# Two layers of a hybrid backbone step on one core: convolution taps dealt anew, pooled sums scaled by ScalarE, row tiles turned through two pairs of PSUM banks

## The reference

```python
h = _rms(x, norm1_g) * (1.0 + sc1) + sh1          # modulation from w_mod
u = h @ w_in                                      # 1024 -> 2048
qa, ka, va, pool_in, glu_in, qd, kd, vd = split(u)
# B: for windows w = 2, 4, 8, 16 on 64 channels each
mean = (cs[:, hi + 1] - cs[:, lo]) / (hi - lo + 1)
o_b = concat((mean - pool_in) @ pool_w) * pool_scale
# C: 31 taps along the tokens, per channel
g = a * sigmoid(gate)
y = conv(g, conv_dw_w, width=31) + conv_dw_b
o_c = silu(layer_norm(y)) @ conv_pw
x = x + g1 * (concat(o_a, o_b, o_c, o_d) @ w_out)  # o_a, o_d: attention
```

## Time and profile before

| | |
|---|---|
| median of 3 runs | 2039.86 us |
| lowest and highest | 2038.81 and 2039.9 us |
| the profiled execution | 2038.71 us |
| its span | 2036.9 us |
| mean granted TensorE clock | 0.935 |
| busy: PE, PEld, DVE, ACT, POOL | 85%, 67%, 29%, 25%, 14% |
| moved | 533.77 MB, 262 GB/s in the mean |

### The profile page before, as it was taken

The page is one execution under the profiler, slowest core; times in us unless marked ns, Lnnn a source line. Parts: engine busy times, 40 slices in busy tenths (PEclk is TensorE's granted clock), DMA queues, the critical chain, the costliest instruction groups (busy, mean ns, idle before and its releaser), DMA issues.

```text
span 2036.9 us, 65158 instructions
## 1 busy us (share of the span) xinstructions
PE 1726.2 (85%) x29816; PEld 1373.7 (67%) x29816; DVE 582.2 (29%) x971; ACT 518.6 (25%) x1286; POOL 289.2 (14%) x292
## 2 busy tenths in 40 slices
PE   4999889984999888888769968999379998989894
PEld 2555466453999888888735535655279998888884
DVE  2168466242111101011123774742501110101011
ACT  2122366111221212121221315641122121212212
POOL 1166200000000000000011680000000000000001
PEclk7999889986999999999979978999589999999997
DMA  9220911247999999999950228012369999999996
GB/s 391 105 83 0 364 59 43 83 171 256 376 388 392 395 389 400 389 400 390 400 200 1 83 92 329 2 63 93 117 243 381 395 393 388 400 388 399 388 396 257
DMA packets 136647, 533.77 MB, mean 262 GB/s; under 512 B 5888, under 2 KB 6976, under 8 KB 136320
## 3 DMA queue, kind: packets, MB, share of 16 engines
q1 hardware_dynamic: 121616, 482.53, 60.3%
q0 software_dynamic: 6336, 21.63, 4.5%
q10 hardware_dynamic: 8624, 28.61, 3.8%
HBM read 508.33 MB, written 24.41 MB: 262 GB/s over the span
## 4 chain that ended last, share of the span: by engine, by line
PE 44%; DMA 32%; SPq 9%; DVE 7%; issue 4%; ACT 2%; POOL 2%; ACTq 0%; POOLq 0%; DVEq 0%; PEldq 0%; PEld 0%
DMA ring<-in_exp_w_down 16%; PE PS L752 13%; SPq L345 9%; PE PS L672 7%; DMA ring<-in_exp_w_up 5%; PE PS L506 4%; DMA x_rows<-arena 4%; DMA arena<-xn_rows,arena 4%; DMA ring<-in_w_mod 3%; PE PS L565 3%; PE PS L582 2%; PE PS L477 2%; PE PS L478 2%; DVE arena L1201 1%; PE PS L411 1%
## 5 line engine op out<-in xcount | busy, mean ns | idle before, releaser
L752 PE MATMUL PS<-arena,ring 128*64 128x80 f32 x24576 | 898.2, 233 | 97.4 <-DMA ring<-in_exp_w_up 41.6
L752 PEld LDWEIGHTS PS<-arena,ring 128*64 128x64 f32 x24576 | 876.7, 137 | 121.3 <-DMA ring<-in_exp_w_up 48.4
L1039 ACT ACTIVATE arena<-PS,modB,modA 128x64 f32<-128x64 f32 (+1 forms) x544 | 153.5, 421 | 405.6 <-PE PS L738 405.6
L1560 POOL DMA_INDIRECT x_rows<-arena x32 | 45.7, 1429 | 756.6 <-DVE arena L1410 756.6
L672 PE MATMUL PS<-ring,H 128*128 128x512 f32 x320 | 139.2, 593 | 0.0
L1397 DVE TENSOR_TENSOR arena<-arena,PS 128x320 f32<-128x320 f32 x64 | 31.4, 490 | 326.1 <-PE PS L752 326.1
L672 PEld LDWEIGHTS PS<-ring,H 128*128 128x128 f32 x320 | 60.0, 190 | 71.9 <-issue 71.7
L506 PE MATMUL PS<-H,ring 128*128 128x512 f32 x192 | 104.6, 628 | 3.4 <-ACT H L826 3.4
L1051 ACT ACTIVATE arena<-PS 128x320 f32<-128x320 f32 x32 | 14.0, 438 | 346.0 <-PE PS L752 346.0
L1201 DVE SCALAR_TENSOR_TENSOR arena<-arena,par 128x655 f32<-128x655 f32 x72 | 99.0, 1375 | 2.2
L1268 DVE TENSOR_REDUCE stat<-PS 128x2 f32<-128x1280 f32 (+1 forms) x54 | 75.5, 1400 | 62.0 <-PE PS L552 53.5
(11 more groups left out here) (191 smaller groups left out, 1733.9 us busy)
## 6 DMA issues: line engine op xcount, KB each, us to landing
ring<-in_exp_w_down SPq DMA_DIRECT2D x64, 2048.0 KB, 26.5
ring<-in_exp_w_gate SPq DMA_DIRECT2D x64, 2048.0 KB, 24.6
ring<-in_exp_w_up SPq DMA_DIRECT2D x64, 2048.0 KB, 25.0
ring<-in_w_mod SPq DMA_DIRECT2D x24, 2048.0 KB, 18.3
ring<-in_w_in SPq DMA_DIRECT2D x8, 2048.0 KB, 27.6
ring<-in_w_out SPq DMA_DIRECT2D x4, 2048.0 KB, 22.6
arena<-x_rows ACTq DMA_DIRECT2D x15, 512.0 KB, 6.7
x_rows<-arena ACTq DMA_DIRECT2D x10, 512.0 KB, 2.6
```

Source lines behind the costliest of these rows:

```text
L752: last = mm(PS[r0:r0 + HD, b0 + j // 4, (j % 4) * CAP:(j % 4 + 1) * CAP], halves[:, s, k * 512 + (j % 4) * P + r0:k * 512 + (j % 4) * P + ...
L1039: last = do(xeT[:, jj, c0:c1], PS[:, 6 + part, j * CAP + c0:j * CAP + c1], ACT.Identity, bias=modB[:, 1, v, jj:jj + 1], scale=modA[:, 1, v ...
```

## The change

Four things. The taps (c) and products (k) are dealt anew in TAKE_ORDER; their number stays 38 and 24. In layer 1 the first pooling moves behind the root of tile 4. The scaling of the pooled sums goes from GpSimd to ScalarE, which waits for the sums (pool_sums) and answers (pool_scaled). Row tiles 1 and 3 of layer 0 and tile 1 of layer 1 are turned into banks 5 and 6, and a tile waits only for the last use of its own pair.

```diff
+        pool_sums, pool_scaled = sem("pool_sums"), sem("pool_scaled")
...
-                uses = [0]
+                uses, last_use = [0], {0: 0, 5: 0}
...
                     uses[0] += 1
+                    last_use[0] = uses[0]
...
                     pe.wait_ge(n_xn, NT * l + t + 1)
-                    banks01(l)
+                    if last_use[XBANK[l][t]]:
+                        pe.wait_ge(b0_evac, 10 * l + last_use[XBANK[l][t]])
+                        pe.wait_ge(b1_evac, 10 * l + last_use[XBANK[l][t]])
+                    uses[0] += 1
+                    last_use[XBANK[l][t]] = uses[0]
                     for j in range(KD):
-                        last = tr(PS[:, j // 4, (j % 4) * P:(j % 4 + 1) * P], xt[t][:, j * P:(j + 1) * P],
+                        last = tr(PS[:, XBANK[l][t] + j // 4, (j % 4) * P:(j % 4 + 1) * P], xt[t][:, j * P:(j + 1) * P],
...
+                def scale_pool(i):
+                    act.wait_ge(pool_sums, 2 * l + i + 1)
+                    for rows, src in ((slice(0, HD), wa), (slice(HD, P), wb)):
+                        last = do(poolD3[rows, i, :], src[rows, PAD:PAD + OUTW], ACT.Copy, scale=invw[rows, i:i + 1])
+                    last.then_inc(pool_scaled, 1)
...
+                    elif kind == "p" and n == 0:
+                        scale_pool(0)
...
+                scale_pool(1)
                 take_mod(l, 3, mix_rows[1], 0)
...
-                    for rows, src in ((slice(0, HD), wa), (half, wb)):
-                        last = G.tensor_scalar(poolD3[rows, i, :], src[rows, PAD:PAD + OUTW], invw[rows, i:i + 1],
-                                               None, ALU.mult)
-                    link(last)
+                    pool.sem_inc(pool_sums, 1)
+                    reach(pool_scaled, 2 * l + i + 1)
...
-               ("p", 0), ("f", 2), ("f", 3), ("c", 5), ("f", 4), ("f", 5), ("m", 2), ("k", 6), ("c", 8), ("j", 0),
-               ("k", 5), ("c", 6), ("q", 0), ("j", 1), ("k", 5), ("c", 6), ("q", 1), ("j", 2), ("k", 5), ("c", 6),
-               ("q", 2), ("j", 3), ("k", 3), ("c", 6), ("q", 3), ("j", 4), ("c", 1), ("f", 1), ("p", 1), ("q", 4)),
+               ("p", 0), ("f", 2), ("f", 3), ("c", 7), ("f", 4), ("f", 5), ("m", 2), ("k", 6), ("c", 11), ("j", 0),
+               ("k", 5), ("c", 5), ("q", 0), ("j", 1), ("k", 5), ("c", 5), ("q", 1), ("j", 2), ("k", 5), ("c", 5),
+               ("q", 2), ("j", 3), ("k", 3), ("c", 5), ("q", 3), ("j", 4), ("f", 1), ("p", 1), ("q", 4)),
...
-               ("z", 0), ("j", 1), ("f", 2), ("f", 3), ("c", 2), ("q", 1), ("c", 6), ("f", 4), ("f", 5), ("m", 2),
-               ("k", 7), ("c", 9), ("j", 2), ("k", 9), ("c", 8), ("f", 0), ("q", 2), ("j", 3), ("k", 8), ("c", 6),
-               ("q", 3), ("p", 0), ("j", 4), ("c", 4), ("f", 1), ("p", 1), ("c", 3), ("q", 4)))
+               ("z", 0), ("j", 1), ("f", 2), ("f", 3), ("c", 2), ("q", 1), ("c", 11), ("f", 4), ("f", 5), ("m", 2),
+               ("k", 9), ("c", 13), ("j", 2), ("k", 9), ("c", 7), ("f", 0), ("q", 2), ("j", 3), ("k", 6), ("c", 5),
+               ("q", 3), ("j", 4), ("p", 0), ("f", 1), ("p", 1), ("q", 4)))
...
+XBANK = ((0, 5, 0, 5, 0), (0, 5, 0, 0, 0))
```

More of the change, by code:

```diff
@@ L825, in step_x @@
                     for j in range(4):
-                        last = do(H[:, j, t * P:(t + 1) * P], PS[:, 0, j * P:(j + 1) * P], ACT.Identity,
+                        last = do(H[:, j, t * P:(t + 1) * P], PS[:, XBANK[l][t], j * P:(j + 1) * P], ACT.Identity,
                                   bias=modB[:, 0, v, j:j + 1], scale=modA[:, 0, v, j:j + 1])
@@ L1134, in step_x @@
                     for j in range(4):
-                        last = V.tensor_scalar(H[:, 4 + j, t * P:(t + 1) * P], PS[:, 1, j * P:(j + 1) * P],
+                        last = V.tensor_scalar(H[:, 4 + j, t * P:(t + 1) * P], PS[:, XBANK[l][t] + 1, j * P:(j + 1) * P],
                                                modA[:, 0, v, 4 + j:5 + j], modB[:, 0, v, 4 + j:5 + j],
```

## The result

The changed kernel took 2012.26 us in the median of four runs (2006.2 to 2018.0), the kernel before 2039.34 beside it: a ratio of 0.9873, 95% interval 0.986 to 0.9887. The profiled execution took 2013.42, its span is 2011.6, 25.3 less than before.

The account below looks back on a forecast made before the run. The prediction took the two input stages to be bound by engines, not loads. Gains of 6.6, 3.6, 1.4 and 13.5 summed to 25.1 us, from 2038.71 to 2013.6, stated as 2014.2 us, range 2009 to 2021.

Parts of the forecast that it names:

- Row tiles, layer 0: Layer 0's input stage: tiles 1 and 3 in banks 5 and 6 overlap turning and emptying, gaining 6.6 us.
- I take no: Layer 0: denser row tiles don't keep TensorE's clock up, so f 0 starts at the half level; 2.6 us stay lost.
- a full clock at f 0: Sign in layer 0's first input projection step that would show the prediction wrong; it expected the half level, 0.50.
- The rival with 9.9: Layer 0: clock holds through the row tiles, 2.6 us more from f 0 and 0.7 from tiles; 2010.9 us, chance 0.12.
- The bound from the emptyings alone: Layer 0's row tiles: five emptyings of 1.51 us back to back end at 47.8, 7.3 us less than 55.23.
- Taps, layer 0: One tap fewer in three intervals before rotation 3: 1.9 us of TensorE waiting plus 1.7 of clock, 3.6 together.
- Row tile, layer 1: Layer 1's input stage: tile 1 in other banks starts earlier, gaining 1.4 us, between 0 and 1.94.
- Tail: End of layer 1's input stage: q 4 11.6 us earlier, loads 1.9 more; 13.5 us, from 11.0 to 14.1.
- Scale: Scaling pooled sums on ScalarE: in layer 1 its wait lies inside that for the loads; 0 us in total.
- Carrying gains to the end: Both input stages: ending earlier by some time should bring the kernel's end forward by as much; terms sum to 25.1 us.
- The new wait on ScalarE: Rival, layer 1: ScalarE waits for GpSimd's sums before emptying f 1, taking part of the tail; 2020.8 us, chance 0.14.
- The slower case: Expert loops on TensorE lie elsewhere and wait at issue, 32 x 1.1 = 35 us lost; 2049 us, chance 0.03.

Follow-up runs that it names:

- e1: Changed kernel with all of layer 0's row tiles turned in banks 0 and 1 again; 2019.69 us, ratio 0.991.
- e7: Changed kernel with only row tile 1 of layer 0 left in the second pair of banks; 2018.69 us, ratio 0.9907.
- e12: e1 with ten more transposes, whose results nothing reads, behind each row tile of layer 0; 2115.38 us, ratio 1.0392.
- e2: Changed kernel with layer 0's taps dealt as before the change; 2015.43 us, ratio 0.9891.
- e9: The kernel before the change, source unchanged, profiled a second time; 2038.2 us, ratio 0.9998.
- e11: Changed kernel with layer 1's row tile 1 in banks 0 and 1 again; 2013.44 us, ratio 0.988.
- e5: e3 with layer 1's first pooling put ahead of tile 4's projection again; 2021.24 us, ratio 0.9921.
- e6: Changed kernel with layer 1's taps and products dealt as before, the first pooling still behind tile 4's root; 2014.08 us, ratio 0.989.
- e3: Changed kernel with the pooled sums scaled on GpSimd again, without ScalarE's handoff; 2011.57 us, ratio 0.9871.
- e8: Changed kernel with layer 1's row tile 3 turned into banks 2 and 3; 2008.07 us, ratio 0.9857.
- e4: Changed kernel with two more no-operations before each loop of experts; 2012.11 us, ratio 0.9874.

## Why the prediction was right, and where it was not

The forecast, 2014.2 in a range of 2009 to 2021, held; both measured medians lie 2 to 3 us below it. The mechanisms that it named were there, but one term was read wrongly and one step was left out, and that the two nearly cancelled was luck.

**Row tiles, layer 0: 6.6 was too small.** j 0 came 10.3 us earlier (95.14 against the row below of the kernel before; 9.8 in the second pair of profiles), and e1 loses 9.7 at the issue.

```profile
105.48 1.10 PE L477 MATMUL PS<-ring,H 128*128 128x512 f32 x2 [0.76 <-issue]
```

Of the 10.3, 8.0 stand before f 0's start, where the full clock of the tiles is part of it, and 2.4 behind it. The step that failed is "I take no": f 0 did not start at the half level, and a full clock at f 0 was one of the prediction's own signs of being wrong. The rival with 9.9 had it, at a chance of 0.12. I read the fall at the third tile as what transposes do; e7 and e12 show that it goes with the waits between them. The bound from the emptyings alone (end at 47.8) was right: f 0 starts at 47.25. The Trainium skill (TensorE: Matmul & The Clock Gate, Part 4: PE-mode transpose), on which that step leaned, says that transposes don't count as TensorE activity in the way that matmuls do. This trace does not agree: in e12 nothing but transposes, with waits of 0.5 to 0.6 us between them, fills 37.78 to 50.8 us, and f 0 begins at the full level (1.12). That transposes alone would also raise a clock that is down, no run here shows.

**Taps, layer 0: 3.6, measured 3.3 to 3.8** (14.15 less 10.34 in the first pair of profiles; 3.3 in e2, and in e9, from j 0 on). The size was right, the split of 1.9 and 1.7 was not: e2 and e9 kept their clock and lost the rest in VectorE's wait before q 4.

**Row tile, layer 1: 1.4, measured 1.4** at the tile (e11), of which some 0.6 is left at the second step of j 0, and nothing that the end can show.

**Tail: 13.5, measured 13.3** (1234.72 to 1212.96, less the 8.46 by which tile 3's sums, 1169.50 before and 1161.04 after, were already early). q 4 gained 11.3 of 11.6, the loads 2.0 of 1.9. e5 and e6 split it by cause: the pooling's place 7.7, the taps and products 3.1 at q 4 and 0.9 at the loads. The 1.6 that is missing to 13.3 shows in neither run alone.

**Scale: 0**, by e3, and by the mechanism that the text gave: the wait lies inside the loads.

**Carrying gains to the end** is the step that the sum left out. I said that an input stage that ends earlier by some time brings the end forward by as much. The two input stages gained 25.7 us, and layer 0's attention and loop lost 3.4 of it in the profiles, while layer 1's loop gave 2.3 back; whether any of this is the change's doing, the scatter of those stages leaves open. In e1 and e8, too, what the stage lost or won (9.7; 4.9 to 6.4) shows at the end as 7.9 and 2.9, with 3 us of interval on each. The sum came out near for two reasons: the row tiles of layer 0 gave 3.2 to 3.7 us more than forecast, for the most part by their clock, and about as much is missing elsewhere (some 0.8 of the row tile of layer 1, and in the stages behind 1.4 lost in sum where the loads had promised 2.0 more).

**The rivals.** The new wait on ScalarE is there (7.47 us of idleness) and costs nothing. The slower case, TensorE's loop in a worse place, did not come about with the few instructions of this change (e4), but e12 shows that such a loss exists: some 6.9 us a pass in layer 0 (591.9 over 15 passes, 39.5 us, against 32.6), above the 4.5 from which I had it decide. My argument against it, a steady loop without issue time, shows only that the loop lay well where it was. The Trainium skill (Runtime: NRT & Kernel Launch, Instruction fetch mechanics) has a taken branch to code outside the window fetched anew. The 41 instruction packets in 300 us of e12 would fit that; but the changed kernel, whose loop is as long, moved none in the same stretch, and what makes one place good and another bad no run here shows.

## What to carry to other kernels

Where TensorE turns tiles one after the other through one PSUM buffer, a second buffer can gain more than the overlap: the waits between the tiles go, and the clock stays up for the tiles and for what comes behind. Here that was worth about 4.3 of 9.1 us (e12), and it held in seven of nine profiles. A pipelined tail is best read from the wait that ends last (here VectorE's for a root on GpSimd), since moving one block of GpSimd's work past it was worth 7.7 us and dealing the taps and products anew 4. Whoever adds instructions ahead of a long loop should look at issue time inside the loop, and should not expect the end to repeat, or to follow a gain, more closely than the stages with the changing clock do.

## What the runs showed that I had not expected

- Fp32 transposes alone kept the clock up (e12), and with waits of 1.6 to 2.2 us between them it came down (e1, e7), in the two profiles of the kernel before at the third tile and at the fourth. Dense tiles don't assure it: in two of the nine profiles with layer 0's dense tiles (e5, e8) f 0's first pair took 1.58 and 1.76 us, in the others 1.12 or 1.13.
- A stage with much waiting, attention, takes 231.3 to 235.3 us in layer 1 and 234.2 to 236.7 in layer 0 in executions of kernels that have the same program there; in the two profiles of the changed kernel its granted clock in layer 1 was 0.94 with 231.3 us and 0.91 with 235.1. Four executions of the changed kernel lay as far apart as 2006.2 and 2018.0, so a single profile can't settle a few us of the whole.
- A hundred instructions ahead of a loop added 103 us to it (591.9 less 488.8), with passes of 30 to 47 us where those of the other loops take 30 to 34.
